# Value projections computed with tokens on the partitions, and the gated heads' chunk recurrence spread over eight pieces, in a hybrid mLSTM and GLA decoder step

## The reference

```
h = rmsnorm(x, g_norm1) * (1 + scale1) + shift1          # scale, shift, gate from c @ w_ada
z = h @ w_in          # q|k, v, o, i, f of the mLSTM; q, k, v, r, low rank of the GLA; two gates
qk = silu(causal_conv4(qk_a));  ha = mlstm(q, k, v, i, f)    # 4 heads, 128 keys, 256 values
hb = gla(q_b, k_b, v_b, log_sigmoid(lr @ w_alpha + b_alpha) / 16)   # 4 heads, 128 keys, 256 values
y = (sigmoid(g_a) * norm(ha) * sigmoid(o_a) + sigmoid(g_b) * norm(hb) * silu(r_b)) @ w_out
x = x + gate1 * y
x = x + gate2 * ((silu(h2 @ w_ffn_gate) * (h2 @ w_ffn_up)) @ w_ffn_down)
```

## Time and profile before

| | |
|---|---|
| median of 3 runs | 1898.91 us (1897.11 to 1906.35) |
| the profiled execution, its own time | 1900.39 us |
| its span, first to last instruction | 1898.2 us |
| mean clock granted to TensorE | 0.989 of full |
| busy: PE, PEld, DVE, ACT, POOL | 1850.8, 1768.3, 1062.2, 701.2, 730.7 us |
| mixer phase, on PE | about 58 to 1058 us |
| from HBM, into HBM | 130.96 MB, 21.50 MB |

### The profile page before, as it was taken

One profiled execution on the slowest core, in us unless ns is written; L12 is line 12 of the kernel. 1 busy time (PEld: TensorE's weight loads), 2 busy tenths in 40 slices (PEclk: granted clock), 3 DMA queues, 4 the chain that ended last, 5 costly groups with the idle time before them and its releaser, 6 DMA issues.

```text
span 1898.2 us, 35239 instructions
## 1 busy us (share of the span) xinstructions
PE 1850.8 (98%) x14123; PEld 1768.3 (93%) x14123; DVE 1062.2 (56%) x1877; ACT 701.2 (37%) x1449; POOL 730.7 (38%) x631
## 2 busy tenths in 40 slices
PE   7899999999999999999999999999999999999998
PEld 5899998999989999889998999999999999999998
DVE  6731653415544236533174778886665666566666
ACT  4543433334333343342354545232233223322327
POOL 4212332313332223323143774443454445434545
PEclk8999999999999999999999999999999999999999
DMA  9331231422312322223232642111121112111212
GB/s 321 104 96 51 76 84 51 132 62 70 90 51 70 112 80 74 57 78 110 76 108 75 227 141 69 56 46 34 46 67 51 40 45 67 48 43 46 68 40 97
DMA packets 190825, 154.73 MB, mean 82 GB/s; under 512 B 10324, under 2 KB 171284, under 8 KB 190152
## 3 DMA queue, kind: packets, MB, share of 16 engines
q1 hardware_dynamic: 190362, 152.27, 26.8%
q10 hardware_dynamic: 302, 0.22, 0.0%
HBM read 130.96 MB, written 21.50 MB: 80 GB/s over the span
## 4 chain that ended last, share of the span: by engine, by line
PE 84%; DVE 8%; issue 3%; POOL 2%; ACT 2%; DMA 0%; ACTq 0%; DVEq 0%; POOLq 0%; SPq 0%
PE bank L984 36%; PE bank L2224 19%; PE bank L2193 12%; PE bank L2091 2%; PE bank L1113 2%; PE bank L1115 1%; PE bank L1118 1%; PE bank L1020 1%; PE bank L2058 1%; PE bank L1156 1%; POOL mix L1418 1%; PE bank L1092 1%; DVE y_rows L2838 1%; PE bank L339 1%; PE bank L1137 1%
## 5 line engine op out<-in xcount | busy, mean ns | idle before, releaser
L1364 POOL TENSOR_TENSOR w_lo<-w_raw,w_hi 128x512 fp32r<-128x512 f32 x128 | 192.9, 1507 | 602.1 <-ACT w_hi L1171 602.1
L984 PE MATMUL bank<-h_hi,w_hi 128*128 128x352 f32 x1536 | 328.8, 336 | 1.3 <-ACT w_hi L1171 1.3
L984 PE MATMUL bank<-h_hi,w_lo 128*128 128x352 f32 x1536 | 313.1, 326 | 2.0 <-POOL w_lo L1364 2.0
L984 PE MATMUL bank<-h_lo,w_hi 128*128 128x352 f32 x1536 | 312.4, 325 | 0.0
L984 PEld LDWEIGHTS bank<-h_hi,w_hi 128*128 128x128 f32 x1536 | 257.4, 190 | 18.6 <-issue 13.9
L984 PEld LDWEIGHTS bank<-h_hi,w_lo 128*128 128x128 f32 x1536 | 259.9, 189 | 3.5 <-POOL w_lo L1364 3.5
L984 PEld LDWEIGHTS bank<-h_lo,w_hi 128*128 128x128 f32 x1536 | 259.9, 189 | 0.0
L2523 POOL TENSOR_TENSOR f_lo<-w_raw,f_hi 128x512 fp32r<-128x512 f32 x107 | 144.0, 1351 | 194.4 <-ACT f_hi L2288 194.4
L2523 POOL TENSOR_TENSOR w_lo<-w_raw,w_hi 128x512 fp32r<-128x512 f32 x107 | 144.2, 1353 | 152.1 <-ACT w_hi L2288 152.1
L2872 DVE SCALAR_TENSOR_TENSOR x_t<-bank,ada,x_t 128x352 f32<-128x352 f32 (+1 forms) x288 | 156.0, 568 | 54.8 <-PE bank L2193 38.3
L1171 ACT ACTIVATE w_hi<-w_raw 128x512 fp32r<-128x512 f32 x128 | 80.4, 628 | 147.1 <-PE bank L984 147.0
(11 more groups left out here) (520 smaller groups left out, 3829.6 us busy)
## 6 DMA issues: line engine op xcount, KB each, us to landing
w_raw<-in_w_in SPq DMA_DIRECT2D x128, 256.0 KB, 2.9
w_ada_tile<-in_w_ada SPq DMA_DIRECT2D x32, 512.0 KB, 4.0
w_raw<-in_w_out SPq DMA_DIRECT2D x48, 256.0 KB, 3.0
w_raw<-in_w_ffn_gate SPq DMA_DIRECT2D x44, 256.0 KB, 3.0
w_raw<-in_w_ffn_up SPq DMA_DIRECT2D x44, 256.0 KB, 3.0
w_raw<-in_w_ffn_down SPq DMA_DIRECT2D x44, 256.0 KB, 2.8
w_ada_ring<-in_w_ada SPq DMA_DIRECT2D x10, 512.0 KB, 9.2
x_scratch<-x_turned_rows SPq DMA_DIRECT2D x1, 4224.0 KB, 16.3
```

What stands on the lines that cost most here:

```text
L984: last = pe.matmul(g.ps[b][:, 0:n], x[:, s, k, :], y[:, 4 * h + k, c0:c0 + n], start=(h == 0 and k == 0 and m == 0), stop=(h == 1 and k == ...
L1364: pool.tensor_tensor(Wl[:, s], raw[:, r], Wh[:, s].bitcast(F32), ALU.subtract).then_inc(s_lo, 1)
```

## The change

- The tile order changes. S: small, q, k, v0, v1 (v0 and v1 come last). A and B: q, v0, v1, k, o0, g0, o1, g1 (k comes after both v).
- For v0 and v1 the operands swap: 128 tokens of `Hh` or `Hl` are the stationary operand and 256 columns of `Wh` or `Wl` move. Each half now holds 256 columns of 2 contraction blocks in place of 128 columns of 4 (`w_half`, `by_two`). The four halves accumulate into the same four piece banks (`mm_values`), two chunks of 128 tokens in each; slots c=0, 1, 2 do 3, 3 and 2 chunks, six matmuls per chunk. ACT copies the four banks into `V` in the last half (`values`).
- The 32 sample tokens no longer go through the three-product split: `vs0` and `vs1` multiply float32 sample rows (`HK`) by the `raw` weights, one contraction block per partition group, ACT copies the first, DVE adds the second, and `vsum` adds the four groups by `gsum`. SP keeps `raw` until these have read it.
- `vt0` and `vt1` and ACT's copies to `VS` go.
- In S, k uses `KD` in place of `Z`, so that it need not wait for q's `silu`.
- In B, `conv_k` goes from slot 20 to 24 (behind `level5` and `level6` in place of ahead of them), `taps_k` from 24 to 26 (behind `level7`), `silu_k` from 30 to 31 (behind `keys`), and the chunks from 31, 31, 32, 32, 32, 33, 34, 35 to 31 to 38.

```diff
-TILES = {"S": ["small", "q", "v0", "k", "v1"],
-         "A": ["q", "v0", "k", "v1", "o0", "g0", "o1", "g1"],
-         "B": ["q", "v0", "k", "v1", "o0", "g0", "o1", "g1"],
+TILES = {"S": ["small", "q", "k", "v0", "v1"],
+         "A": ["q", "v0", "v1", "k", "o0", "g0", "o1", "g1"],
+         "B": ["q", "v0", "v1", "k", "o0", "g0", "o1", "g1"],
          "L": ["o0", "g0", "o1", "g1"]}
...
+    "S": [("rows", 8), ("conv_q", 16), ("taps_q", 16), ("rows_exp", 17), ("silu_q", 19), ("vs0", 20), ("rows_t", 21), ("conv_k", 23),
+          ("taps_k", 24), ("silu_k", 25), ("decay_load", 25), ("interq_load", 25), ("vs1", 26), ("vsum", 27)],
...
-    "B": [("ada_load0", 3), ("conv_q", 7), ("taps_q", 8),
-          ("silu_q", 10), ("ada0", 14), ("level3", 14), ("ada_load1", 15), ("level4", 16), ("vt0", 16), ("conv_k", 20),
-          ("level5", 20), ("level6", 22), ("ada1", 22), ("taps_k", 24), ("level7", 26), ("ada_load2", 27), ("vt1", 27),
-          ("silu_k", 30), ("masked", 30), ("keys", 30), ("chunk0", 31), ("chunk1", 31), ("chunk2", 32), ("chunk3", 32),
+    "B": [("ada_load0", 3), ("conv_q", 7), ("taps_q", 8), ("vs0", 8), ("silu_q", 10), ("ada0", 14), ("level3", 14), ("vs1", 14),
+          ("vsum", 15), ("ada_load1", 15), ("level4", 16), ("level5", 20), ("level6", 22), ("ada1", 22), ("conv_k", 24),
+          ("level7", 26), ("taps_k", 26), ("ada_load2", 27), ("masked", 30), ("keys", 30), ("silu_k", 31), ("chunk0", 31),
+          ("chunk1", 32), ("chunk2", 33), ("gate_r0", 33), ("decay_load", 33), ("chunk3", 34), ("chunk4", 35), ("gate0", 35),
...
+    if name[0] == "v":
+        n = 2 * int(name[1]) + h
+        return w_in[:, 2 * n:2 * n + 2, bass.ds(head * step + base, DV)]
...
+                        if c == 0 and TILES[w][l][0] == "v":
+                            wait_use(sp, w, i, USE[w]["vs" + TILES[w][l][1]])
...
+            def mm_values(w, i, l, h, c):
...
+                for t in range(3 * c, min(3 * c + 3, NC)):
+                    b, turns = piece(w, i, v0, t // 2)
+                    if n == 0 and t % 2 == 0:
+                        wait(pe, s_pfree[b], turns)
+                    for m, (x, y) in enumerate(((g.Hh, Wh), (g.Hl, Wh), (g.Hh, Wl))):
+                        if t == 0 and m == 2:
+                            pe.wait_ge(s_lo, before + 1)
+                        for k in range(2):
+                            last = pe.matmul(g.ps[b][:, t % 2 * DV:(t % 2 + 1) * DV], x[:, 2 * n + k, t * P:(t + 1) * P],
+                                             by_two(y[:, s])[:, k, :], start=(n == 0 and k == 0 and m == 0 and t % 2 == 0),
+                                             stop=(n == 3 and k == 1 and m == 2 and t % 2 == 1))
...
-                    elif name in ("vt0", "vt1"):
-                        wait_evacuated(pe, w, i, TILES[w].index("v" + name[2]))
-                        turned(n, VS)
+                    elif name in ("vs0", "vs1"):
+
+                        l = TILES[w].index("v" + name[2])
+                        pe.wait_ge(s_hi, half(w, i, l, 1)[3] + 1)
+                        pe.wait_ge(s_dve, 1)
+                        bank = use(n)
+                        for j in range(NG):
+                            r = half(w, i, l, j // 2)[0]
+                            last = pe.matmul(bank[NS * j:NS * (j + 1), 0:DV], HK[:, NG * int(name[2]) + j, :], by_two(raw[:, r])[:, j % 2, :],
+                                             start=True, stop=True)
+                        full(last)
+                    elif name == "vsum":
+                        wait_read(pe, w, i, "vs1")
+                        bank = use(n)
+                        for j in range(NG):
+                            last = pe.matmul(bank[NS * j:NS * (j + 1), 0:DV], g.gsum[:, :], VP, start=True, stop=True)
+                        full(last)
...
-                elif name[0] == "v":
-                    last = act.activation(VS[:, c0:c0 + n], src, ACT.Copy)
...
+            def values(w, i, bank):
...
+                wait_values(act, w, i, bank)
+                act.activation(V[0 if w in "SB" else 1][:, 2 * bank:2 * bank + 2, 0:DV],
+                               g.ps[b][:, :].rearrange("p (c d) -> p c d", d=DV), ACT.Copy).then_inc(s_pfree[b], 1)
...
+                        if TILES[w][l] == "v1" and h == 1:
+                            for bank in ((0,), (1, 2), (3,))[c]:
+                                values(w, i, bank)
...
+                    elif name == "vs1":
+                        wait_read(dve, w, i, "vs0")
+                        wait_use(dve, w, i, n)
+                        dve.tensor_tensor(VP, VP, RB(n)[:, 0:DV], ALU.add).then_inc(free(n), 1)
```

More of the change, by code:

```diff
@@ L560, in _, with pieces_before @@
                 lower(2 * s + 1)
-TILES = {"S": ["small", "q", "v0", "k", "v1"],
-         "A": ["q", "v0", "k", "v1", "o0", "g0", "o1", "g1"],
-         "B": ["q", "v0", "k", "v1", "o0", "g0", "o1", "g1"],
+TILES = {"S": ["small", "q", "k", "v0", "v1"],
+         "A": ["q", "v0", "v1", "k", "o0", "g0", "o1", "g1"],
+         "B": ["q", "v0", "v1", "k", "o0", "g0", "o1", "g1"],
          "L": ["o0", "g0", "o1", "g1"]}
 NS_TILES, NW_TILES = len(TILES["S"]), len(TILES["A"])
+NV_BANKS = NC // 2
+PIECES_OF = {"v0": NV_BANKS, "v1": 0}
+def pieces_before(w, l):
+    return sum(PIECES_OF.get(name, NPC) for name in TILES[w][:l])
+NS_PIECES, NW_PIECES = pieces_before("S", NS_TILES), pieces_before("A", NW_TILES)
 COLUMN = {("A", "q"): (C_QB, DK), ("A", "k"): (C_KB, DK), ("A", "v"): (C_VB, DV), ("A", "o"): (C_OA, DV), ("A", "g"): (C_GA, DV),
@@ L575 @@
 AT_SLOT = {
-    "S": [("rows", 8), ("conv_q", 16), ("taps_q", 16), ("rows_exp", 17), ("silu_q", 19), ("rows_t", 21), ("vt0", 21),
-          ("conv_k", 23), ("taps_k", 24), ("silu_k", 25), ("decay_load", 25), ("interq_load", 25), ("vt1", 29)],
-    "A": [("decay", 1), ("ada_load0", 2), ("alpha_hi", 3), ("alpha_lo", 9), ("scores", 6), ("keys", 6), ("interq", 8),
[19 rows of a table removed]
+    "S": [("rows", 8), ("conv_q", 16), ("taps_q", 16), ("rows_exp", 17), ("silu_q", 19), ("vs0", 20), ("rows_t", 21), ("conv_k", 23),
+          ("taps_k", 24), ("silu_k", 25), ("decay_load", 25), ("interq_load", 25), ("vs1", 26), ("vsum", 27)],
+    "A": [("decay", 1), ("ada_load0", 2), ("alpha_hi", 3), ("scores", 6), ("keys", 6), ("interq", 8), ("vs0", 8), ("alpha_lo", 9),
[7 rows of a table added]
+          ("level7", 26), ("taps_k", 26), ("ada_load2", 27), ("masked", 30), ("keys", 30), ("silu_k", 31), ("chunk0", 31),
[9 rows of a table added]
 }
-USES = {"scores": 3, "keys": 3, "vt0": 3, "vt1": 3, "sample_out": 1, "turn0": 3, "turn1": 3,
+USES = {"scores": 3, "keys": 3, "vs0": 1, "vs1": 1, "vsum": 1, "sample_out": 1, "turn0": 3, "turn1": 3,
         "alpha": 3, "rows_t": 3, **{s: 2 for s in CHAIN}, **{s: NG for s in SAMPLE}, **{f"ada{q}": 1 for q in range(4)}, "adas": 1,
@@ L680, with by_two @@
 RAW = 4
+def by_two(v):
+    return v.rearrange("p (a b) c -> p a (b c)", a=2)
 def w_half(w_in, w, i, l, h):
@@ L799, in piece @@
         def piece(w, i, l, c):
[L800 to L804, removed]
+            per = 2 * NW_PIECES
+            k, j = pieces_before(w, l) + c, 0
+            if w != "S":
+                k, j = k + NS_PIECES + (NW_PIECES if isB(w) else 0), i
             return static(j, per, k, 4)
@@ L820, in wait_piece, with wait_values @@
                 e.wait_ge(s_used, half(w, i, l, 1)[3] + 1)
+        def wait_values(e, w, i, bank):
+            if bank < NV_BANKS - 1:
+                e.wait_ge(s_piece, tile_index(w, i, TILES[w].index("v0")) * 2 + (bank + 2))
+            else:
+                e.wait_ge(s_used, half(w, i, TILES[w].index("v1"), 1)[3] + 1)
         def wait_evacuated(e, w, i, l):
@@ L989, in mm_piece @@
                     last.then_inc(s_piece, 1)
+            def mm_values(w, i, l, h, c):
+                _, s, _, before = half(w, i, l, h)
+                v0 = TILES[w].index("v0")
+                n = 2 * (l - v0) + h
+                if c == 0:
+                    pe.wait_ge(s_hi, before + 1)
+                for t in range(3 * c, min(3 * c + 3, NC)):
[9 more added lines that the diff above has]
+                                             stop=(n == 3 and k == 1 and m == 2 and t % 2 == 1))
+                    if n == 3 and t % 2 and t < NC - 1:
+                        last.then_inc(s_piece, 2 if t == 1 else 1)
+                if c == 2:
+                    last.then_inc(s_used, 1)
             def window(w, i):
@@ L1235, in window @@
                                 out_hi(act, n)
-                        if h == 1:
+                        if TILES[w][l] == "v1" and h == 1:
+                            for bank in ((0,), (1, 2), (3,))[c]:
+                                values(w, i, bank)
+                        elif h == 1 and TILES[w][l] != "v0":
                             evacuate(w, i, l, c)
@@ L1273, in window @@
                         act.wait_ge(s_cv, m)
[L1274 to L1284, removed]
```

(11 more changed lines are left out.)

47 lines of the change are left out of this document (33 added, 14 removed), and 26 rows, old and new, of the table AT_SLOT.

## The result

The changed kernel takes 1879.22 us (median of five runs, 1878.49 to 1889.26), beside 1898.91 for the kernel before (1897.11 to 1906.35). The medians are 19.7 us apart. The quotient of the medians is 0.9896; the measured ratio, with its 95% interval, is 0.9907 [0.9887, 0.9926]: faster by about 1%. Two more series of the same kernel gave 0.9898 [0.9881, 0.9914] and 0.9907 [0.9892, 0.9922]. The profiled execution took 1879.22 us (span 1877.0, mean clock 0.995), 21.2 less than that of before, where the prediction's sum was 24.5.

The account below looks back on a forecast made before the run. The prediction took PE, busy 98% of the span, as the bound. Gains of 8.8 + 14.1 + 1.6 = 24.5 us take 1900.4 to 1875.9, given as a 1874.4 us median; likeliest case 1867 to 1882, with bounds and neighbouring cases 1862 to 1889.

Parts of the forecast that it names:

- PE is the bound, and its matmuls cost 0.46 ns a column: Whole kernel: PE busy 98% of the span; projection matmuls cost 0.46 ns per column with nearly nothing fixed.
- rivals that hung on this price, at 0.107 and at 0.134 or more: Value matmuls of 256 columns: at 0.107 us about 1857 in all (chance 0.12); from 0.134 on, slower (chance 0.05).
- Value part, 1.1 us a head: Value projections, turning removed, sample stages added: gain 1.1 us a head, between 0.3 and 3.9, 8.8 over 8 windows.
- Window B's order, 4.7 us each: Three windows B: conv_k later lets level6 start earlier; stop, short waits and slow matmuls give back 4.7 us each, 14.1 together.
- The stop shrinks to 1.0 us: PE's wait ahead of the level6 matmuls in window B falls from 2.92 to 1.0 us and does not vanish.
- The clock stays: Behind window B's level6 stop of 1.0 us the clock would not fall and would read 1.00.
- the stop stays, half clock with it: Rival, chance 0.16: window B's stop at level6 and half clock remain; gain only 10.4 us, 1888.5.
- `silu_k` behind `keys`, slack 0.5: Window B: silu_k at slot 31 leaves 0.5 us of slack before chunk1; failing costs 1 us three times.
- Spreading them gives nothing and costs nothing: Window B, one chunk per slot: zero gain and zero cost on PE; ACT and DVE get more room.
- Window S, 1.6 and 1.1: Window S: 1.6 us from waits for a bank and for ACT going, plus 1.1 from the value part.
- The rest of the trace ... as before and 24 us earlier: From the FFN phase on, the profile after would be unchanged, only 24 us earlier.
- The sum: 8.8 value part, 14.1 window B's order and 1.6 window S make 24.5 us; chance 0.62 of 1867 to 1882.

Follow-up runs that it names:

- order-alone run: Kernel before with only window B's conv_k moved to slot 24 and taps_k to 26, behind level5 and level6: 1888.03 us, ratio 0.9944.
- run with the difference later: Changed kernel with one extra value-neutral DVE instruction ahead of the difference for level6 in windows B: 1883.56 us, ratio 0.9920.
- packed chunks: Changed kernel with window B's chunks at their old slots (31, 31, 32, 32, 32, 33, 34, 35), silu_k still behind keys: 1881.71 us, ratio 0.9918.
- kernel with all edits: Changed kernel with level6 at 23, POOL's side at 22 (B); level5 at 7, level6 at 9 (L); rows_exp at 18, vsum at 29 (S): 1869.55 us.

## Why the prediction was right, and where it was off

*PE is the bound, and its matmuls cost 0.46 ns a column.* Right, also at 256 columns, which no row of before had: 0.118 us, the value on the line. The rivals that hung on this price, at 0.107 and at 0.134 or more, are out.

*Value part, 1.1 us a head.* 1.2 by the order-alone run. The tiled rounds took 0.50 to 0.57 and 0.2 for the return, for 0.6 and 0.2. By the Trainium skill ("TensorE: Matmul & The Clock Gate", section on packing small matmuls) one round would have been 0.44, an estimate; the trace has more, 0.50 to 0.57, inside the bounds of 0.43 to 0.65. Eight heads give 9.8 for 8.8.

*Window B's order, 4.7 us each.* 4.1 each, so 12.4 for 14.1, and the term that was mis-sized is the stop: "The stop shrinks to 1.0 us", where it measured 1.7. The place, the releaser and the sign were right. The steps behind it, on DVE and POOL:

```profile
275.64 1.26 DVE L1769 TENSOR_TENSOR temp_b<-temp_a 128x1056 f32<-128x1056 f32 x1 [3.83 <-POOL k_decayed L1475]
...
280.30 2.07 DVE L1628 TENSOR_TENSOR q_decayed<-q_b,temp_b 128x528 f32<-128x528 f32 x1
```

```profile
278.80 1.28 POOL L1440 TENSOR_TENSOR w_lo<-w_raw,w_hi 128x512 fp32r<-128x512 f32 x1 [3.26 <-ACT w_hi L1239]
280.05 1.76 POOL L1472 TENSOR_TENSOR k_decayed<-q_b,k_b 128x528 f32<-128x528 f32 x1
281.76 2.00 POOL L1475 TENSOR_TENSOR k_decayed<-k_b,temp_b 128x528 f32<-128x528 f32 x1
```

The difference starts 6.5 us ahead of PE's arrival at 282.18 (before: 285.72 - 280.80 = 4.9), so 1.6 earlier, for 1.8 in the prediction (2.2 less the 0.4 by which PE comes earlier). The prediction let POOL's L1399 of `level5` shrink to 1.3 us; its successor L1475 takes 1.55 there, which is what the earlier trace rows has for it (1.52) where DVE stands still. And from the difference to PE's start are 283.86 - 275.64 = 8.2 us, for the 7.8 of before, which I had kept. POOL's two instructions of the k side take 3.8 us together instead of the 3.0 that the earlier trace rows has (1.52 each), L1440 0.35 less than it did. They now lie beside DVE's L1628, which takes 2.07 there. At `level5` of the same window the same two lines, on the same shapes, each run while the other engine stands still; first DVE's, then POOL's:

```profile
271.11 0.71 DVE L1628 TENSOR_TENSOR q_decayed<-q_b,temp_b 128x528 f32<-128x528 f32 x1 [0.36 <-ACT temp_b L1424]
```

```profile
273.99 1.55 POOL L1475 TENSOR_TENSOR k_decayed<-k_b,temp_b 128x528 f32<-128x528 f32 x1
```

Side by side, then, DVE's goes from 0.71 to 2.07 and POOL's from 1.55 to 1.76 and 2.00. Two runs took the neighbour away at `level6` itself. With `level6` one slot later, DVE was done before POOL began, and all three run at their lengths alone (L1472, shown there, 1.56); DVE, then POOL:

```profile
280.42 0.70 DVE L1628 TENSOR_TENSOR q_decayed<-q_b,temp_b 128x528 f32<-128x528 f32 x1
```

```profile
285.22 1.53 POOL L1475 TENSOR_TENSOR k_decayed<-k_b,temp_b 128x528 f32<-128x528 f32 x1
```

The run with the difference later has 0.70, 1.53 and 1.53, so the chain from the difference to PE is 0.25 shorter there, which is why its stop grew by less than the delay. The Trainium skill ("GPSIMD Engine Reference", section on key points) says that GpSimd shares its SBUF interfaces with VectorE and contends with DVE instructions that read two inputs, and these rows agree. The trace of before has a neighbour of the other kind: L1364 takes 1.29 us (at 275.71) wholly beside DVE's L1438, which reads one tile, and as much alone; right behind it L1399 takes 2.05 beside L1439, which reads two. DVE itself is slowed with one input too: its copy L1626 takes 0.85 us beside POOL in the changed kernel and 0.44 in the run with the difference later. So the start of the difference accounts for 0.2 and POOL's lengths for 0.4 of the 0.7; the last 0.1 is that PE starts 0.1 behind POOL's end, which the prediction left out. The prediction moved a chain earlier and took its durations along; the neighbours on the other engine change with the move.

*The clock stays.* Right for the profiled execution, in part by luck: the reason given ("A wait of 1.78 in window L ... left it at 1.00 behind it") was one observation of a thing that varies. Behind that same wait of L the clock fell in 3 of the 11 profiles that have it (at a cost of 0.1 us only, since the next wait then vanished). In nine profiles with a stop of 1.6 to 1.9 at `level6` the clock fell behind 4 of 27. So the rival "the stop stays, half clock with it" lives on as a small tax: 4 / 27 x 3 x 1.5 = 0.7 us per execution as an estimate, and in S, where the fall came in 3 of 8 profiles for 1.4, another 0.5. It accounts for a part of the distance between executions of the same kernel.

*`silu_k` behind `keys`, slack 0.5.* Right, and shown by the packed chunks, which lose the slack and pay 1.1 a period. But "Spreading them gives nothing and costs nothing" was wrong as it stood: beside the old `silu_k` it may hold, beside the new one the spreading is worth 1.0 to 1.1 in each period. The prediction did not see that its one sentence hangs on the other.

*Window S, 1.6 and 1.1.* 2.9 for 2.7. The waits for the bank and for ACT went, `vsum` did not wait, and its cover was as thin as said.

*"The rest of the trace ... as before and 24 us earlier".* Off by 2.7 us in that execution. It is not tied to the change as far as the runs can say: over the thirteen profiles of this study, setup ends at 57.7 to 59.8 and `w_out` with the FFN takes 838.6 to 844.2, and the kernel before (58.13 and 840.02) lies inside both. The packed chunks had 838.55, and the kernel with all edits 844.21. The traces show most of what it is made of. Up to PE's last instruction, the FFN phase takes 832.5 us where the clock never falls in it (the packed chunks), 834.0 to 834.9 with 3.4 us at half clock (six profiles, both kernels among them), 835.3 to 836.9 with 6.8 (four) and 838.6 with 10.2 (two); from there to the end of the span are 4.4 to 7.6 us more. Of the 1.6 us between the first two profiles 0.6 lie ahead of PE's last instruction and 1.1 behind it (7.1 for 6.0), and the 1.1 of setup is idle time of PE, 13.6 for 12.5. Why these vary stays open. It is also why a comparison of single spans can't tell 2 us, and that of the same window in each trace can.

*The sum.* 23.9 us in the mixer phase for 24.5 is closer than its parts: window B's order gave 1.7 less than forecast and the value part, as the difference puts it, 1.0 more. That these nearly cancel is luck.

## What to carry to other kernels

When one engine is full and the others are half empty, go by its stops, and ask of each which instruction on another engine ended last and what stood ahead of that in the engine's order: moving a convolution of about 4 us behind the chain gave 4.1 us in each of three windows, and moving only POOL's part ahead of the rest gave the other 1.6, while moving the whole stage gave nothing. When you move such a chain, take its durations from rows with the neighbours that it will have, not from those that it had. And read the gain phase by phase at marks that both traces have, since the phases you did not touch scatter by more than the small terms of your sum.

## What the runs showed of the hardware

- *The granted clock behind a stop of PE is not the same from one execution to the next.* Stops ahead of `level6` of 2.9 us: the clock fell to 0.50 behind 3 of 3 in the profile of before. Of 2.6 to 2.7: 2 of 3. Of 1.6 to 1.9: 4 of 27. Ahead of `level5` in window L, 1.8 us: 3 of 11. In S, where two waits of 1.2 to 1.3 and 1.0 lie 1.3 us apart: 3 of 8; behind the one of 3.03: 1 of 1. Where it falls in B or S, it costs 1.4 to 1.7 us (48 matmuls in 9.46 for 7.97). A single profile can't tell that a stop is harmless.
- *A moving column costs the same at 256, 264 and 352 columns*: 0.118, 0.122 and 0.162 us for an fp32r matmul on a full PE, no floor down to 256.
- *Four float32 matmuls of 256 columns in four column groups* take 0.50 to 0.57 us together, and the first full matmuls behind them 0.2 more.
- *Two-input products of 128x528 that run at once* lengthen on both engines: POOL's from 1.55 to 1.76 and 2.00 us, DVE's from 0.71 to 2.07. With DVE done before POOL begins, the same three take 0.70, 1.56 and 1.53.
